# A two-block transformer kernel on one core: the second block's attention part in a new order of weight chunks

## The reference, cut to what matters

```python
ada = (c_act @ w_ada + b_ada)              # 6 x 2048 numbers: shifts, scales, gates
h = _rms(x, g_norm1) * (1 + sc1) + sh1
proj = h @ w_in                            # c_q 512, c_kv 512, k_pe 64, q_sb k_sb v_sb 3 x 1024, gl_a gl_b 2 x 2048
q = _rms(c_q, g_q_latent) @ w_uq           # 8 heads of 192
kv = _rms(c_kv, g_kv_latent) @ w_ukv       # 8 heads of 128 + 128
q, k = _rms(q, g_q_head), _rms(concat(k_nope, k_pe), g_k_head)   # then rope on the last 64 of each
y_a = _mla_attention(q, k, v)              # causal softmax
y_b = _stick_breaking(q_sb, k_sb, v_sb)    # exp(log_sigmoid(z) + cumulated log_sigmoid(-z))
merged = sigmoid(gl_a) * (y_a @ w_proj_mla) + sigmoid(gl_b) * (y_b @ w_proj_sb)
x = x + gt1 * (merged @ w_out)
```

## Time and profile before

| | |
|---|---|
| median of 3 runs | 2860.98 us (2859.38 to 2862.79) |
| profiled execution, own time | 2857.69 us |
| its span | 2855.9 us |
| mean granted PE clock | 0.979 |
| DMA, mean over the span | 204 GB/s |

### The profile page before, as it was taken

One profiled execution on the slowest core, in us unless ns is written; L12 is line 12 of the kernel. 1 busy time (PEld: TensorE's weight loads), 2 busy tenths in 40 slices (PEclk: granted clock), 3 DMA queues, 4 the chain that ended last, 5 costly groups with the idle time before them and its releaser, 6 DMA issues.

```text
span 2855.9 us, 35410 instructions
## 1 busy us (share of the span) xinstructions
PE 2711.3 (95%) x12421; PEld 2232.9 (78%) x12421; DVE 1753.8 (61%) x2043; ACT 1292.7 (45%) x1510; POOL 3.2 (0%) x9
## 2 busy tenths in 40 slices
PE   8999999999999999996999998789989999999998
PEld 6888887778888878785887777567768888887877
DVE  5776668777667767775644444556567644444555
ACT  5555544444444434344545455443354444444433
POOL 0000000000000000000000000000000000000000
PEclk9999999999999999998999999899999999999999
DMA  7655546788877878783765554234568766564554
GB/s 252 209 154 150 153 141 224 256 284 278 285 269 272 279 258 294 245 278 116 231 213 164 158 172 130 74 110 147 177 206 281 262 191 185 187 189 153 191 162 162
DMA packets 302065, 581.32 MB, mean 204 GB/s; under 512 B 19916, under 2 KB 20292, under 8 KB 301716
## 3 DMA queue, kind: packets, MB, share of 16 engines
q1 hardware_dynamic: 300896, 576.34, 62.4%
q10 hardware_dynamic: 740, 2.27, 0.2%
q0 software_dynamic: 336, 1.46, 0.2%
HBM read 577.89 MB, written 2.10 MB: 203 GB/s over the span
## 4 chain that ended last, share of the span: by engine, by line
PE 88%; DVE 6%; ACT 3%; issue 2%; DMA 1%; ACTq 0%; DVEq 0%; SPq 0%
PE acc L326 27%; PE acc L327 27%; PE acc L328 27%; DVE lo L315 2%; PE ex L960 1%; PE aux L982 1%; ACT hi L309 1%; PE tp L1347 1%; PE aux L523 1%; DVE op_lo L453 1%; DMA raw<-w_out 0%; PE tp L433 0%; PE aux L1998 0%; DVE op_hi L452 0%; ACT stage L445 0%
## 5 line engine op out<-in xcount | busy, mean ns | idle before, releaser
L315 DVE TENSOR_TENSOR lo<-raw,hi 128x1024 fp32r<-128x1024 f32 x895 | 1075.2, 1222 | 571.3 <-ACT hi L309 545.4
L309 ACT ACTIVATE hi<-raw 128x1024 fp32r<-128x1024 f32 x895 | 923.8, 1055 | 659.3 <-PE acc L328 480.6
L326 PE MATMUL acc<-hi,op_hi 128*128 128x512 f32 x2872 | 1144.1, 398 | 54.8 <-DVE lo L315 49.5
L327 PE MATMUL acc<-lo,op_hi 128*128 128x512 f32 x2872 | 1127.1, 392 | 0.0
L328 PE MATMUL acc<-hi,op_lo 128*128 128x512 f32 x2872 | 1126.8, 392 | 0.0
L326 PEld LDWEIGHTS acc<-hi,op_hi 128*128 128x128 f32 x2872 | 544.8, 190 | 179.4 <-issue 45.9
L328 PEld LDWEIGHTS acc<-hi,op_lo 128*128 128x128 f32 x2872 | 544.3, 190 | 116.4
L327 PEld LDWEIGHTS acc<-lo,op_hi 128*128 128x128 f32 x2872 | 545.3, 190 | 108.6 <-issue 0.2
L326 PE MATMUL acc<-hi,f_hi 128*128 128x512 f32 x704 | 282.4, 401 | 19.3 <-issue 11.9
L327 PE MATMUL acc<-lo,f_hi 128*128 128x512 f32 x704 | 280.7, 399 | 0.0
L328 PE MATMUL acc<-hi,f_lo 128*128 128x512 f32 x704 | 280.4, 398 | 0.0
(11 more groups left out here) (279 smaller groups left out, 1196.2 us busy)
## 6 DMA issues: line engine op xcount, KB each, us to landing
raw<-w_in SPq DMA_DIRECT2D x257, 512.0 KB, 3.9
ada_ring<-w_ada SPq DMA_DIRECT2D x192, 512.0 KB, 5.2
raw<-w_gate_up SPq DMA_DIRECT2D x176, 512.0 KB, 4.9
raw<-w_ffn_in SPq DMA_DIRECT2D x176, 512.0 KB, 4.6
raw<-w_down SPq DMA_DIRECT2D x88, 512.0 KB, 5.9
raw<-w_ffn_out SPq DMA_DIRECT2D x88, 512.0 KB, 4.3
raw<-w_out SPq DMA_DIRECT2D x64, 512.0 KB, 5.0
raw<-w_proj_sb SPq DMA_DIRECT2D x16, 512.0 KB, 3.7
```

The lines of the kernel that those rows point to most:

```text
L309: A.activation(hi[:, k, :, 0:n], raw[:, k, :, 0:n], ACT.Copy).then_inc(hi_ready, 1)
L315: V.tensor_tensor(lo[:, k, :, 0:n], raw[:, k, :, 0:n], hi[:, k, :, 0:n].bitcast(F32), ALU.subtract).then_inc(lo_ready, 1)
L326: T.matmul(dst, lh, hi[:, k, kk, 0:n], start=first and kk == 0, stop=False)
L327: T.matmul(dst, lh, lo[:, k, kk, 0:n], start=False, stop=False)
```

## The change

The six stages are replaced by one list of 207 chunks, numbered G, and each engine has one unrolled stream over it (sp_second, act_second, dve_second, pe_second). The order is: the two latent blocks (G 0 to 15), k_pe (16), the first stick column block (17 to 24), the up-projections (G_UP = 25, 14 chunks), the other five stick column blocks (G_SB = 39, 40 chunks), the gates (G_GATE = 79, 64 chunks), the two projections alternating by output block (G_PP = 143, 32 chunks), and the out-projection (G_OUT = 175, 32 chunks). The same chunks are multiplied, none more and none less.

The latents' norm and transposes stand at G 16 to 23, the norms and rope of q beside the up-projections, the key norm at G 41. The four mla groups start at G 44, 53, 62 and 71 (mla_at), beside stick columns, nine chunks each; the four stick groups start at G 79, 95, 111 and 127 (stick_at), beside gates, sixteen chunks each. The readout of a block stands on ACT (on DVE from G_PP on) three chunks behind its last one. The steps of a group keep their instructions and get new places: for a stick group PE 3, 5, 8, 11, ACT 2, 6, 8, 11, 14 and DVE 6, 8, 11, 12 after its start; for an mla group PE 0, 2, 5, 7, ACT 2, 3, 5, 6 (the fetch of the next group), 8 and DVE 3, 5, 6, 10. The projections' product is gated by DVE block by block, and the merged operand is transposed in pairs from G_PP + 9 on. The latents, y_a and y_b get buffers of their own; k's gain is multiplied into q's (one instruction on 192 columns), which takes away L1853; the constants are loaded in two parts by POOL.

Outside the second block, modulation groups 1 and 2 move from out1 to the recurrence's groups 0 and 1 (ADA_REC), at chunks 5, 7, 9, 11, 13, 15, 20 and 21 of each.

The diff, cut to its core:

```diff
@@ -728,6 +743,8 @@
                 for k in range(RC):
                     c0 = REC[g][k // 8][0]
                     sp_chunk(sp, rec_chunk(g, k), 0, 4 * RC, w_in[k % 8][:, :, c0:c0 + NB])
+                    if g < 2 and k in ADA_REC:
+                        sp_ada(sp, A_REC + g, 0, ADA_REC[k], ada_ring0)
 
...
 
         WK = (4, 5, 0, 1, 2, 3, 6, 7)
         LEFT = (((op2_hi, op2_lo), 0), ((op2_hi, op2_lo), 2)) + tuple(((op_hi, op_lo), kt) for kt in (0, 2, 4, 6, 12, 14))
-        ADA_OUT1 = {c: j for j, c in enumerate((8, 9, 10, 12, 13, 14, 16, 17, 21, 22, 24, 25, 26, 28, 29, 30))}
 
         def sp_out1(sp):
             for c in range(32):
@@ -1102,11 +1121,6 @@
...
@@ -910,6 +927,8 @@
                         dve_keep(dve, cd, g, k // 2 - 4)
                     for s in D_AT.get(k, ()):
                         dve_decay(dve, g, s)
+                    if g < 2 and k in ADA_REC:
+                        dve_ada(dve, cd, A_REC + g, 0, ADA_REC[k], ada_ring0)
                     if not last:
...
         CH, BL = {}, {}
         c = b = 0
         for name, nc_, nb_ in (("in1", 32, 4), ("in1b", 96, 0), ("out1", 32, 4), ("gu1", 176, 22), ("dn1", 88, 4),
-                               ("in2", 129, 17), ("up", 14, 7), ("pb", 16, 0), ("pa", 16, 4),
-                               ("out2", 32, 4), ("gu2", 176, 22), ("dn2", 88, 4)):
+                               ("in2", 25, 4), ("up", 14, 7), ("in2b", 40, 5),
+                               ("in2c", 64, 8), ("pp", 32, 8), ("out2", 32, 4), ("gu2", 176, 22), ("dn2", 88, 4)):
             CH[name], BL[name] = c, b
             c, b = c + nc_, b + nb_
...
+        C2 = CH["in2"]
+        G_UP, G_SB, G_GATE, G_PP, G_OUT, G_END = (CH[n] - C2 for n in ("up", "in2b", "in2c", "pp", "out2", "gu2"))
+        PE0 = C_KV + HEADS * (NOPE + VD)
+        SB0 = PE0 + ROPE
+        FREE0 = SB0 + 3 * DH
+        MLA_AT, MLA_PER = G_SB + 5, 9
+        STICK_PER = 16
+
+        def mla_at(g):
+            return MLA_AT + MLA_PER * g
+
+        def stick_at(g):
+            return G_GATE + STICK_PER * g
+
+        def gate_cols(j):
+            c0 = j * NB if j < 7 else FREE0
+            return proj[:, :, c0:c0 + NB]
+
...
+        def sp_second(sp):
+            for G in range(G_END):
+                c = C2 + G
+                if G == 16:
+                    sp.wait_ge(lo_ready, c - RING + 1)
+                    sp.dma_start(all_tiles(raw, c), a["w_in_2"][0].rearrange("(k p) n -> p k n", p=P)[:, :, C_PE:C_SB]).then_inc(raw_ready[c % RING], 16)
+                elif G < G_UP or G_SB <= G < G_PP:
+                    sp_chunk(sp, c, 0, 4, in2_src(G))
+                elif G < G_SB:
+                    sp_chunk(sp, c, 0, 4, up_src(G - G_UP))
+                elif G < G_OUT:
+                    sp_chunk(sp, c, 0, 4, pp_src(G - G_PP))
+                else:
+                    sp_chunk(sp, c, 0, 4, out2_src(G - G_OUT))
+                if G - 8 in ADA_AT and G < G_UP:
+                    if ADA_AT[G - 8] == 0:
+                        sp.wait_ge(norm_ready, 8)
+                    sp_ada(sp, A_IN2, 0, ADA_AT[G - 8], ada_ring3)
+
+
+        B2 = BL["in2"]
+
+        def bank2(n):
+            return (B2 + n) % 2
+
...
+            return (B2 + n) // 2 + 1
+
+
+        ENDS = {7: 0, 15: 1, 16: 2, 24: 3}
+        ENDS.update({G_UP + 2 * b + 1: 4 + b for b in range(7)})
+        ENDS.update({G_SB + 8 * s + 7: 11 + s for s in range(5)})
+        ENDS.update({G_GATE + 8 * j + 7: 16 + j for j in range(8)})
+        ENDS.update({G_PP + 4 * j + 3: 24 + j for j in range(8)})
+        ENDS.update({G_OUT + 8 * b + 7: 32 + b for b in range(4)})
+        END_OF = {n: G for G, n in ENDS.items()}
+
...
+        def act_stick(act, g, at):
+            if at == 2:
+                if g == 0:
+                    act.wait_ge(ml["o"], GROUPS)
+                    act.wait_ge(acc_free[bank2(15)], freed2(15))
+                else:
+                    act.wait_ge(sk["o"], g)
+                src = proj[:, :, SB0:FREE0].rearrange("p t (d n) -> p t d n", d=3)[:, :, :, g * GW:(g + 1) * GW]
                 for t in range(TT):
                     A.activation(s_in[:, t], src[:, t], ACT.Copy).then_inc(sk["in"], 1)
-            if k == 7:
+            if at == 6:
                 act.wait_ge(sk["tr"], g + 1)
                 A.activation(s_qk[:, :, 0:S], tp[:, :, 0:S], ACT.Copy, scale=float(P) ** -0.5).then_inc(sk["q"], 1)
-            if k == 10:
+            if at == 8:
                 act.wait_ge(sk["z"], g + 1)
...
+            merged = lambda g: act_operand(act, OG["merged"], 8, None, only=[g])
+            for G in range(G_END):
+                if G < 8:
+                    h2(G)
+                act_chunk(act, C2 + G, 0, 4)
+                n = ENDS.get(G - 3)
+                if n is not None:
+                    if n < 2:
+                        act_read2(act, n, proj[:, :, n * LAT:(n + 1) * LAT], ACT.Copy)
+                        act_latent_squares(act, n)
+                        if n == 1:
+                            act_latent_root(act)
+                    elif n == 2:
+                        done2(act, 2)
+                        A.activation(shared[0:ROPE], acc[0:ROPE, bank2(2), 0, 0:S], ACT.Copy).then_inc(acc_free[bank2(2)], 1)
+                    elif n == 3:
+                        act_read2(act, n, proj[:, :, SB0:SB0 + NB], ACT.Copy)
+                    elif n < 11:
+                        if n == 4:
+                            act.wait_ge(lt["split"], LG)
+                        act_read2(act, n, proj[:, :, (n - 4) * NB:(n - 3) * NB], ACT.Copy)
+                    elif n < 16:
+                        act_read2(act, n, proj[:, :, SB0 + (n - 10) * NB:SB0 + (n - 9) * NB], ACT.Copy)
+                    elif n < 24:
+                        act_read2(act, n, gate_cols(n - 16), ACT.Sigmoid)
+                if G == 14:
+                    act_angles(act)
+                if 19 <= G < 19 + LG:
+                    act_latent(act, G - 19)
+                if G == 24:
+                    act_pe(act)
+                if G == G_UP + 8:
...
+                        merged(2 * j + G - (G_PP + 12 + 8 * j))
+                if G_OUT + 1 <= G < G_OUT + 5:
+                    merged(4 + G - (G_OUT + 1))
+                if G == G_OUT + 10:
+                    act_row(act, 0)
+
+
+        def dve_angles(dve, cd, part):
             r, n, tmp = m_ang[:, 2], m_ang[:, 3], m_ang[:, 0]
-            if k == 6:
-
-                dve.wait_ge(m_load, 4 * 16)
+            if part == 0:
+                dve.wait_ge(m_load, 2 * 16)
                 cd.done(V.tensor_copy(small[:, 4, 0:TT], m_pos[:]))
...
+        def dve_second(dve, cd, out_readout):
+            merged = lambda g: dve_operand(dve, cd, OG["merged"], 8, 0, only=[g])
+            for G in range(G_END):
+                if G < 8:
+                    dve_operand(dve, cd, OG["h2"], 8, 0, only=[G])
+                dve_chunk(dve, C2 + G, 0, 4)
+                if G in (12, 13, 16):
+                    dve_angles(dve, cd, (12, 13, 16).index(G))
+                if G == 18:
+                    dve_latent_root(dve, cd)
+                if 20 <= G < 20 + LG:
+                    j = G - 20
+                    dve.wait_ge(lt["ev"], CK * (j + 1))
+                    dve_split_to(cd, lat_hi[:, CK * j:CK * j + CK], lat_lo[:, CK * j:CK * j + CK], latent(j), lt["split"])
+                if G - 8 in ADA_AT and G < G_UP:
+                    dve_ada(dve, cd, A_IN2, 0, ADA_AT[G - 8], ada_ring3)
+                if G == G_UP + 3:
...
+        def pe_mla(pe, g, at):
+            if at == 0:
                 pe.wait_ge(ml["in"], g * IN + IN)
-                if later(g):
+                if g:
...
+            if at == 11:
+                pe.wait_ge(sk["a"], g + 1)
+                for h in range(GH_HEADS):
+                    ins = causal_product(aux[:, h], [s_in[:, t, 2, h * P:(h + 1) * P] for t in range(TT)], s_b[:, h])
+                ins.then_inc(sk["o"], 1)
+
+        def pe_merged(pe, g):
+            j = g // 2
...
+        def pe_second(pe, h2):
+            n = 0
+            for G in range(G_END):
+                c, into = C2 + G, acc[:, bank2(n)]
+                if G == 0 or G - 1 in ENDS:
+                    pe_acc_wait(pe, B2 + n, 0, 2)
+                if G < 8:
+                    h2(G)
+                if G == 16:
+                    pe_key_product(pe, c, B2 + n)
+                elif G < G_UP:
+                    k = G % 8 if G < 16 else G - 17
+                    pe_chunk(pe, c, 0, 4, into, CK * k, k == 0, k == 7)
+                elif G < G_SB:
+                    k = (G - G_UP) % 2
+                    kt = CK * k + (0 if G - G_UP < 6 else 4)
+                    pe.wait_ge(lt["split"], kt // 2 + 1)
+                    pe_chunk(pe, c, 0, 4, into, kt, k == 0, k == 1, left=(lat_hi, lat_lo))
+                elif G < G_PP:
+                    k = (G - (G_SB if G < G_GATE else G_GATE)) % 8
```

(82 more changed lines are left out.)

799 lines of the change are left out of this document (343 added, 456 removed).

## The result

The changed kernel takes **2783.64 us**, the median of 4 runs (2782.42 to 2784.18). The kernel before took 2860.18 us beside it (4 runs, 2857.59 to 2862.79). The ratio is **0.9732, 95% interval 0.9715 to 0.9749**: 76.5 us faster. The forecast was 67 us faster, 2794 us, with 2787 to 2803 as its own range and 2782 to 2816 as the wide one.

The account below looks back on a forecast made before the run. PE, busy 2711.3 of 2855.9 us, idles on latency of chains through ACT and DVE. 78.1 - 7.7 new waits - 3.4 clock + 0.5 = 67.5, rounded to 67; 2861.0 - 67 = 2794 us, range 2787 to 2803, chance 0.58.

Parts of the forecast that it names:

- The new waits: Up-projections, key norm and latents' root: crowded ACT and DVE steps make PE wait 1.6 + 2.7 + 0.9 + 2.2 + 0.3 = 7.7 us.
- The margins: Attention groups: chains hide under three chunks (8.2 us), with 1.1 us to spare for stick and 0.4 for mla.
- Rival (a): Attention groups and up: margins of 0.4 to 1.5 us fail, a wait per group stays; 2805 to 2824 us, chance 0.20.
- The table loads: Stick groups on ACT: each load takes 1.28 us, no drain; by the skill's page PE would wait 1.7 us per group.
- 0.5 for the out-projection: First out-projection: moving the modulation away removes 0.5 us of PE's waits for lo.
- Idle time: Rearranged stages: 55.4 us of PE idle in 505 us can go, less 7.7 us of new waits.
- rival (d): Some 90 handshake places: steps one chunk too early cost 2.3 us each; 69 us for thirty, 3001 at worst; chance 0.03.
- Clock: Rearranged stages: 25.7 us lost to lower clock, less 3 already counted as idle and 3.4 falling after remaining waits.
- (c): Recurrence: the moved modulation is not covered, up to 24.5 us back, 2795 to 2818 us; chance 0.06.
- a sign of being wrong: Recurrence: it was to stay 337 us long; the forecast is wrong if it grows.
- (b): Up-projections and key norm: their chain hides too, as other engines start with a fuller lead; 11 us more, 2783; chance 0.10.
- Unrolled code at nothing: Unrolled streams: longer code costs nothing, since the recurrence is unrolled too and keeps PE busy 336.63 of 337 us.

Follow-up runs that it names:

- lag1: Changed kernel with readouts of output banks 3 to 31 one chunk behind the chunk that closes the bank, not three: 2859.93 us, ratio 1.0001.
- lag2: Changed kernel with readouts of output banks 3 to 31 two chunks behind the chunk that closes the bank, not three: 2784.68 us, ratio 0.9742.
- tail7: Changed kernel with PE's running sums of the stick weights one chunk earlier in each of four groups: 2791.07 us, ratio 0.9763.
- mla4: Changed kernel with PE's transposes of the latent attention's weights one chunk earlier in each of four groups: 2795.24 us, ratio 0.978.
- best: Changed kernel with q's gain product and rope one and two steps later, key root and first fetch split, mla groups one chunk later: 2772.71 us.
- ada_only: Kernel before with only modulation groups 1 and 2 moved from the first out-projection into the recurrence: 2856.96 us, ratio 0.9994.
- second_only: Changed kernel with modulation groups 1 and 2 put back into the first out-projection: 2784.4 us, ratio 0.9743.
- lag1b: lag1 with ACT's readout of a closed bank behind the attention step of the same chunk, not ahead of it: 2811.7 us, ratio 0.9837.
- unrolled: Kernel before with the loops of the second block's attention part written out, order of work kept: 2857.48 us, ratio 0.9997.

## Why the prediction was right, and where it was short

**Mechanism: right.** It said that the idle time is latency of chains through ACT and DVE, not lack of their throughput, and that a chain costs nothing once it is shorter than the chunks that PE has in hand. lag1 shows it at its hardest: the same instructions, DVE and ACT as idle as before, and 76 us more. lag2, tail7 and mla4 put the border where the count of chunks in hand puts it. What each piece of the new order gave was not tried by itself; it is read from the list of waits.

**The new waits: each in its place, 6.9 us for 7.7.** The four in the timeline of PE stand at the chunks that were named, 36, 37, 42 and 43, though 113 to 140 us behind the first chunk and not 100 to 125:

```profile
1454.98 0.47 PE L341 MATMUL acc<-hi,lat_hi 128*128 128x512 f32 x1 [1.30 <-DVE lo L330]
...
1460.35 0.47 PE L341 MATMUL acc<-hi,lat_hi 128*128 128x512 f32 x1 [2.33 <-DVE lo L330]
...
1477.02 0.50 PE L341 MATMUL acc<-hi,op_hi 128*128 128x512 f32 x1 [1.14 <-DVE lo L330]
...
1481.88 0.50 PE L341 MATMUL acc<-hi,op_hi 128*128 128x512 f32 x1 [1.82 <-DVE lo L330]
```

1.30, 2.33, 1.14 and 1.82 us, against 1.6, 2.7, 0.9 and 2.2, and 0.3 at the latents. That the list of waits says 7.7 for lo is chance: 1.15 us of it are four short waits at the opening of the block, which the kernel before has too. best removes the four by spreading the steps named as their cause, so the cause is shown.

**The margins held.** s_n was to be 1.1 us early and is 0.86, and 2.15 in the first group; m_s was to be 0.4 early, and the transposes (1507.07) start 0.6 after its last product. Rival (a) was the one to fear: tail7 and mla4, one chunk earlier for one kind of chain, made the block 7.0 and 10.8 us longer.

**The table loads.** The trace shows 1.28 us and the next function 0.01 us later, as the rows before did, and nothing between Abs and the load. The Trainium skill ("ScalarE: Activation LUTs", What ACT_TABLE_LOAD costs) adds a drain of 1.38 us for each switch. As an estimate by that page, PE would wait 1.9 us (2 x 1.38 - 0.86) in three of the four stick groups. No group waits; the measurement decides.

**Where the sum was short: busy time.** The sum had 67.0 us for the second block, before 0.5 for the out-projection; the block gave 73.6, 6.6 more. By terms:
- Idle time: 47.7 forecast (55.4 - 7.7), 49.5 measured. The windows of the earlier trace rows left out the first 218 us of the block, with 2.7 us of idle time: 1.2 in short waits and the first 1.5 of the wait of 4.7 for s_n, which ends at 1566.25. That edge is also why rival (d) found more wait for s_n (14.0) than idle time (13.4) beside the stick attention; it isn't the modelled ends. 12.5 of the 13.4 are for s_n and 0.9 for op_lo.
- Clock: 19.3 forecast (25.7 - 3.0 - 3.4), about 20.6 measured. In the block the trace's clock records have eleven stretches at 1.2 GHz before, behind the one of 3.5 us that opens it in both kernels: 51.2 us together, of which PE was busy 44.6, so 22.3 lost; one such stretch of 3.4 us is left, 1.7.
- The first matmuls behind a wait: 0 forecast. The remainder of the 24.1 us by which busy time fell, 3.5 us, has this as a likely cause in part: at 2.4 GHz the matmul behind a wait keeps the next one 0.31 us off (1454.98, then 1455.29), where the others have 0.23. With 22 waits fewer (9 for 31) that makes about 2 us, an estimate; the other 1.5 us stay open, and no run isolates either.

**Outside the block** the change shows 3.8 us less ahead of it: the block begins at 1345.3 us before and at 1341.5 after. I would have read this as the moved modulation. It isn't. ada_only begins at 1344.9, and second_only, without the move, at 1341.2; the seven kernels that have the same instructions ahead of the block (the changed one, best, lag2, lag1, lag1b, tail7 and mla4) begin at 1341.5 to 1345.9. It is spread between executions. Behind the block the changed kernel's trace has 2.1 us more than before. Of the 76.5 us between the medians 73.6 are thus the block, and the rest is within that spread. The 0.5 us for the out-projection can't be told from it.

**Rivals.** (c) falls: the added DVE work is hidden in the recurrence. But the recurrence did grow, by 1.7 us, which was named as a sign of being wrong: PE's own small products moved there, and the forecast had left them out. (b), 2783 us, has the right time by luck: the up and key chain did not hide, its waits are there, and the missing time came from the terms above. (d) did not come about in the change, but lag1 built it. Its price per place was wrong: a simple readout one chunk behind costs 0.6 us on ACT and 1.0 on DVE, and not 2.3. What makes it dear is the place where a chain with little cover is queued behind the step that waits: 5.39 us each, and four of them weigh as much as 36 plain ones of 0.6.

**Unrolled code at nothing** was right: unrolled shows it with the order kept.

## What to carry to other kernels

When a matmul engine waits now and then for engines that are half idle, write down for each chain when its result is due in chunks, and lay at least its length over it; then look where several steps meet in one chunk and spread them. In an in-order stream, check each waiting step for what is queued behind it: here readouts that came two places too early in the stream cost as much as the whole reordering had gained, and 48 us of those 76 only because steps whose input was ready, an Abs above all, stood behind them. A step placed one chunk later than it must be costs nothing as long as nobody waits for it.

## What the runs showed of the hardware

In these traces the granted clock stayed at 2.4 GHz behind most single short waits of PE and fell around the longest ones. Stretches of 6.8 us just behind a wait, first tail7 (behind 1.76 us), then lag1 (behind 5.39 us):

```profile
1692.30:1699.10 6.80, 6.80 (x38) 5.97 (x39) 5.14 (x5) 5.92 (x6) 0.00 (x0) 1.00 0.53 159
```

```profile
1674.30:1681.10 6.80, 6.78 (x31) 6.21 (x32) 5.09 (x5) 3.77 (x4) 0.00 (x0) 0.74 0.54 172
```

The granted clock is 1.00 in the one and 0.74 in the other: PE had about half of it at 1.2 GHz, and the fall came already inside the wait (at 1671.0 us). All four waits of 5.39 us have such a fall, none of tail7's four for s_n. Between them it goes either way: of mla4's four waits of 2.04 us one is followed by 3.4 us at 1.2 GHz, and of the three of 3.09 us in the kernel before two are.

So a sum of waits doesn't tell the clock's loss. lag1's 46.9 us of added waits came with 27.5 us of added busy time, 22.6 of them by its stretches at 1.2 GHz, 0.48 per us. tail7's 5.9 us of added waits came with 1.1 us of added busy time, 0.2 of it by the clock. The changed kernel's own 8.0 us of waits came with one such stretch, 1.7 us or 0.21 per us, where the forecast had taken 0.45 from the kernel before: that is a mean over its long and short waits, and too high for a list of short ones.
